# First layer of a fused two-block transformer: steps of the convolution and of the gate rows also advance behind the modulation units, and each chain has one step less

## Chip, cores, metric

The kernel runs on one core of one Trainium2 chip. The metric is the device time of one execution in microseconds (us). Before the change the median of three runs is 1377.7 us (1375.81 to 1378.25).

## What is computed

Two transformer blocks work on 256 tokens of width 1024, all in fp32. The first block has two mixers side by side (an attention of 8 heads and an mLSTM of 4 heads) and then a mixture of experts; the second is two layers of attention and a gated feed-forward. Both scale and shift their inputs by "modulation" vectors that come from a small matrix product of a condition `c`. What the change touches is the first block's mixer:

```python
mod = jax.nn.silu(c) @ w_ada[l] + b_ada[l]            # 12 units of 512 columns
sh1, sc1, g1, sh2, sc2, g2 = jnp.split(mod, 6, axis=-1)
h = modulate(x, norm1_g[l], sh1, sc1)
proj = h @ w_in[l]
q_a, k_a, v_a, qk_m, v_m, o_m, gates = jnp.split(proj, offs, axis=-1)
...
qk_m = jax.nn.silu(causal_conv(qk_m, conv_w[l], conv_b[l]))   # width 4
q_m, k_m = jnp.split(qk_m, 2, axis=-1)
gates = gates.astype(jnp.float32) + b_gate[l].astype(jnp.float32)
...
logf = jax.nn.log_sigmoid(f_pre); cum = jnp.cumsum(logf, axis=-1)   # running sums and maxima per head
...
hm = (hm * jax.nn.sigmoid(o_m.astype(jnp.float32))).astype(x.dtype)
```

## The kernel before

Five queues are written in program order: TensorE (PE), VectorE (DVE), ScalarE (ACT) and SyncE (SP, which issues the DMAs); GpSimd does nothing. Each engine runs its queue strictly in order, and waits on semaphores only where an operand or a buffer needs it. So the order in which the Python code emits instructions is the order on each engine.

All weights stream from HBM in units of 2 MB. A ring of four slots holds them; a slot is loaded again as soon as its unit has been consumed (`release`, or the last split of `stage`). The units of the first layer come in this order: modulation units `ada(0, n)` and projection units `U_IN + n` mixed.

A **projection unit** is multiplied with three fp32r products per tile (`mm3`). For that each of its eight slabs of 128 x 512 is split in two: ACT copies the high part (`ACTIVATE memr<-ring`), DVE subtracts for the low part (`TENSOR_TENSOR memr<-ring,memr`). `stage` does this up to four slabs ahead of the one in use (`NSP = 4`). PE then spends six matmuls of 512 columns (or twelve of 256) on the slab, and `slab_done` stages the next one.

A **modulation unit** (`ada_unit`) is 16 PE instructions `ps<-ring,csb`, one copy of the result to `rowb` by ACT, and later four transposes by PE (`ps<-cst,rowb`) and two small DVE instructions (`ada_close`). The transposes of the two open units are emitted behind the third slab of the next projection.

**Side work.** Other work that is not on the straight path is written as Python generators in the list `side`. `slab_done` advances each generator in it by one step, so one step's instructions stand on their queues behind each slab. In the first layer `side` holds `work()`, which goes through `jobs`: `conv(0)`, `conv(1)`, `gate_rows`, and later `mlstm`. `conv(u)` does four channel groups of 128 x 256 (one ACT instruction for the first tap, three on DVE, one SiLU per two). `gate_rows` is a chain of 14 small instructions on DVE and 5 on ACT over 4 x 256 or 4 x 128: biases, log-sigmoid (Exp, Ln), running sums and maxima, and at its end three `Exp` whose records are `gr_["e"]`. The first step of `mlstm` puts three PE transposes (`ps<-cst,mem`, 4 x 4) on PE's queue that wait for `gr_["e"]`. `drain()` emits at once whatever is left in `side`; it is called ahead of `mlstm`, behind the modulation units 7 and 8.

The order of the units around the change is: projection `U_IN + 3` (conv input 0), `U_IN + 4` (conv input 1), gates, modulation 4, `U_IN + 6` (output gate `omT`), modulation 5 and 6, `U_IN + 5` (`vm`), modulation 7 and 8, `drain()`, then `U_IN` (queries of the attention, called q slabs below) with the first steps of `mlstm` behind its slabs.

ACT holds one set of function tables at a time; `use_tables` loads the other set where a function needs it (`ACT_TABLE_LOAD`): SiLU and Tanh are in one, Exp and Ln in the other.

Of the kernel before, what the change touches and what calls it, by code (L numbers as in the profile page):

```python
# [165 lines left out]
def program(nc, t, dbg=None):  # L166
    vt, sc, te, sy, gp = nc.vector, nc.scalar, nc.tensor, nc.sync, nc.gpsimd
    ctx = ExitStack()
    with ctx:
# [154 lines left out]
        side = []  # L324
# [22 lines left out]
        def slab_done(z, rec):  # L347
            sp_free[z] = [rec]
            st["used"] += 1
            stage()  # L350
            for g in list(side):
                if next(g, StopIteration) is StopIteration:
                    side.remove(g)

        for slot in range(RING):
            load_unit(slot, [])
# [42 lines left out]
        def ada_mm(i, n):  # L399

            w, ld = unit("cols")
            src = csb[:, 0 if i == 0 else 1, :, :]
            b, ps, fr = PB.take()
            for k in range(8):
                j = k % 4
                r = mm(ps[32 * j:32 * j + 32, :], src[:, k, :], w[:, k, :], k < 4, k >= 4,
                       after=([ld, cs_r[0 if i == 0 else 1]] + fr) if k == 0 else ())
            release(r)
            ada_made.append((i, n, b, ps, r))
# [11 lines left out]
        def ada_unit(i, n):  # L421

            if len(ada_open) == 2:
                ada_close()
            ada_mm(i, n)
            ada_copy()
# [36 lines left out]
        def project(x2, x_r, evac, order=tuple(range(8))):  # L463

            bk = [PB.take(), PB.take()]
            for kk, k in enumerate(order):
                w, ld, z = slab()
                for tt in range(2):
                    s = slice(128 * tt, 128 * tt + 128)
                    r = mm3(bk[tt][1][:, :], (x2[0][:, k, s], x2[1][:, k, s]), w, kk == 0, kk == 7,  # L470
                            after=bk[tt][2] + [ld, x_r[k]])
                slab_done(z, r)
                if kk == 2:
                    ada_close(True)
            outs = []
            for tt in range(2):
                v = evac(tt, bk[tt][1], [r])
                PB.give(bk[tt][0], [v])
                outs.append(v)
            return outs, r  # L480
# [18 lines left out]
        def project_T(x2, x_r, c1, c2):  # L499
            out = []  # L500
            for _ in project_T_steps(x2, x_r, c1, c2, out):
                pass
            return out

        def silu(dst, src, after):
            use_tables(SILU)
            return A(sc.activation, dst, src, ACT.Silu, after=after)
# [272 lines left out]
        def conv(u, copies):  # L780
            prev, tap = None, {}

            def first(c):
                tap[c] = A(sc.activation, qmT[:, c, :], cT[:, c, 0:256], ACT.Identity, bias=cols[:, C_CB + c:C_CB + c + 1],
                           scale=cols[:, C_CW + 4 * c:C_CW + 4 * c + 1], after=[copies[c % 4 // 2], pad])

            first(4 * u)
            yield
            for c in range(4 * u, 4 * u + 4):
                r = tap[c]  # L790
                for j in (1, 2, 3):
                    r = V(vt.scalar_tensor_tensor, out=qmT[:, c, :], in0=cT[:, c, j:j + 256],
                          scalar=cols[:, C_CW + 4 * c + j:C_CW + 4 * c + j + 1], in1=qmT[:, c, :], op0=ALU.mult, op1=ALU.add,
                          after=[r])
                    if j == 1:
                        if c < 4 * u + 3:
                            first(c + 1)
                        yield
                yield
                if c % 2:  # L800
                    s = qmT[:, c - 1:c + 1, :]
                    conv_r[c] = conv_r[c - 1] = silu(s, s, [prev, r])
                prev = r
# [19 lines left out]
        def gates():  # L823
            b, ps, fr = PB.take()
            for k in range(8):
                r = mm3(ps[0:36, 0:256], (wg2[0][:, k, :], wg2[1][:, k, :]), (h2[0][:, k, :], h2[1][:, k, :]),
                        k == 0, k == 7, after=fr + wg_r + [h2_r[k]])
            return b, ps, r

        def gate_rows(b, ps, r):  # L830
            r1 = V(vt.tensor_scalar, rw[:, IG, :], ps[0:4, 0:256], bg[:, 0:1], None, ALU.add, after=[r, ld_rows])
            r2 = V(vt.tensor_copy, rw[:, FP, :], ps[32:36, 0:256])
            PB.give(b, [r1, r2])
            r2 = V(vt.tensor_scalar, rw[:, FP, :], rw[:, FP, :], bg[:, 1:2], None, ALU.add, after=[r2])
            r = V(vt.tensor_scalar, rw[:, T1, :], rw[:, FP, :], -1.0, None, ALU.mult, after=[r2])
            r = V(vt.tensor_tensor, rw[:, T1, :], rw[:, T1, :], rw[:, FP, :], ALU.max, after=[r])
            yield
            use_tables(LOG_EXP)
            r = A(sc.activation, rw[:, T1, :], rw[:, T1, :], ACT.Exp, scale=-1.0, after=[r])
            r = A(sc.activation, rw[:, T1, :], rw[:, T1, :], ACT.Ln, bias=1.0, scale=1.0, after=[r])  # L840
            yield
            r = V(vt.scalar_tensor_tensor, out=rw[:, T2, :], in0=rw[:, FP, :], scalar=0.0, in1=rw[:, T1, :],
                  op0=ALU.min, op1=ALU.subtract, after=[r])
            yield
            for c in range(2):
                s = slice(128 * c, 128 * c + 128)
                rc = V(vt.tensor_tensor_scan, rw[:, CU, s], cst[0:4, K_ONE:K_ONE + 128], rw[:, T2, s], 0.0, ALU.mult,
                       ALU.add, after=[r, ld_c1])
            yield
            ru = V(vt.tensor_tensor, rw[:, UU, :], rw[:, IG, :], rw[:, CU, :], ALU.subtract, after=[rc, r1])  # L850
            r = V(vt.tensor_tensor_scan, rw[:, MM, 0:128], rw[:, UU, 0:128], rw[:, UU, 0:128], 0.0, ALU.max, ALU.max,
                  after=[ru])
            yield
            r = V(vt.tensor_tensor, m1, rw[:, CU, 127:128], rw[:, MM, 127:128], ALU.add, after=[r])
            rn = V(vt.tensor_scalar, nml, rw[:, MM, 127:128], -1.0, None, ALU.mult)
            r = V(vt.tensor_tensor_scan, rw[:, MM, 128:256], rw[:, UU, 128:256], rw[:, UU, 128:256], m1, ALU.max,
                  ALU.max, after=[r])
            gr_["rM"] = r
            yield
            r = V(vt.tensor_tensor, rw[:, EM, :], rw[:, CU, :], rw[:, MM, :], ALU.add, after=[r])  # L860
            yield
            gr_["e"] = [A(sc.activation, rw[:, EM, :], rw[:, EM, :], ACT.Exp, scale=-1.0, after=[r]),
                        A(sc.activation, rw[:, WP, 0:128], rw[:, UU, 0:128], ACT.Exp, bias=nml, scale=1.0, after=[rn]),
                        A(sc.activation, rw[:, WI, 128:256], rw[:, MM, 128:256], ACT.Exp, bias=m1, scale=-1.0), ru]
            yield
# [202 lines left out]
        copies = conv_copy(0, *conv_out)  # L1068
        jobs = []

        def work():
            while jobs:
                g, n = jobs[0]
                for _ in range(n):
                    if next(g, StopIteration) is StopIteration:
                        jobs.pop(0)
                        break
                yield

        gate_weights()  # L1080
        jobs += [(conv(0, copies), 1)]
        side.append(work())
        bk, r = project_T(h2, h2_r, 256, 128)
        copies = conv_copy(1, bk, r)
        jobs += [(conv(1, copies), 1), (gate_rows(*gates()), 1)]
        if not side:
            side.append(work())
        ada_unit(0, 4)
        bk, r = project_T(h2, h2_r, 256, 128)
        for j in range(2):  # L1090
            o = omT[:, 2 * j:2 * j + 2, :]
# [2 lines left out]
            PB.give(bk[j][0], [ra])  # L1094
            om_r.append(V(vt.tensor_scalar, o, o, 0.5, 0.5, ALU.mult, ALU.add, after=[ra]))
        ada_unit(0, 5)
        ada_unit(0, 6)
        vm_r += project(h2, h2_r, lambda tt, ps, dep: A(sc.activation, vm[:, tt, :], ps[:, :], ACT.Copy, after=dep))[0]
        ada_unit(0, 7)
        ada_unit(0, 8)  # L1100
        drain()
        use_tables(LOG_EXP)
        jobs.append((mlstm(), 1))
        if not side:
            side.append(work())

# [36 lines left out]
        wo1, _ = fold_out(c2_, c_r, (4, 5, 6, 7), 0, 0, x_r)  # L1143
# [452 lines left out]
        for i in (1, 2):  # L1596
# [181 lines left out]
            else:  # L1778
# [64 lines left out]
                _, h2_last = project(h2, h2_r, q_ev(1))  # L1843
# [17 lines left out]
            wo1, _ = fold_out(c2_, c_r, (0, 1, 2, 3), i, 0, x_r)  # L1861
# [16 lines left out]
            for n in range(11):  # L1878
                bk, ff_last = project_T(h2, h2_r, 128, 256)
                for m in range(2):  # L1880
                    f = 2 * n + m
                    z = f % 4
                    b, ps, _ = bk[m]
# [25 lines left out]
            x_r, _ = fold_out(act2, f_r, tuple(range(22)), i, 1, x_r, nm)  # L1909
# [124 lines left out]
```

How the kernel before makes its waits and increments, by code:

```python
def emit(q, ops, seen):  # L133
    for o in ops:
        if o[0] == "wait":
            r = o[1]
            if seen.get(r.sem.name, 0) < r.value:
                q.eng.wait_ge(r.sem, r.value)
                seen[r.sem.name] = r.value
        elif o[0] == "op":
            ins = o[1](*o[2], **o[3])
            if o[4].marked:
                ins.then_inc(o[4].sem, o[4].step)
        elif o[0] == "load":
            q.eng.reg_load(o[1], o[2])
        else:
            with q.eng.If_cmp(o[1], o[2], "IS_GT"):
                emit(q, o[3], dict(seen))
```

## Time and profile before

| quantity | value |
|---|---|
| median of three runs | 1377.7 us (1375.81 to 1378.25) |
| profiled execution: its time | 1377.22 us |
| its span in the trace | 1375.4 us |
| PE busy | 1153.6 us (84%) |
| DVE busy | 611.5 us (44%) |
| ACT busy | 540.8 us (39%) |
| read from HBM | 394.97 MB, 288 GB/s over the span |
| mean granted TensorE clock | 0.944 of full speed |

The span begins with the first instruction and ends with the last; about 1.8 us of the profiled execution's time lie outside it. The mean share says little by itself: the program has stages with different limits, and the stage of the change ends some 100 us after the start.

### The profile page before, as it was taken

How to read it: one execution, taken by the hardware profiler on the slowest of the kernel's cores; microseconds unless marked ns; L12 is line 12 of the kernel's file. 1: busy time of each engine (PE TensorE's matmuls, PEld its weight loads, DVE VectorE, ACT ScalarE, POOL GpSimd, SP SyncE). 2: the span in 40 equal slices, each digit the busy share in tenths (PEclk: the TensorE clock that was granted, in tenths of full speed). 3: DMA queues.
4: the chain of work that ended last, by engine and by line, in shares of the span. 5: the costliest groups of instructions: out<-in, count | busy, mean ns of one | idle time of the engine just before them, and what ended most of it. 6: DMA issues, size and time to landing. Idle time of an engine off the chain costs nothing.

```text
span 1375.4 us, 22370 instructions
## 1 busy us (share of the span) xinstructions
PE 1153.6 (84%) x9627; PEld 917.0 (67%) x9627; DVE 611.5 (44%) x1363; ACT 540.8 (39%) x1203; POOL 0.2 (0%) x4
## 2 busy tenths in 40 slices
PE   6989998857475666657589989999999989999997
PEld 4867678534243443424257757999998758899997
DVE  4564664201110110101165765665555855655554
ACT  4554553211101111101155665555554654655553
POOL 0000000000000000000000000000000000000000
PEclk9999998989788889978899999999999999999999
DMA  9895847899999999999978655555546655655520
GB/s 390 345 356 223 355 186 294 341 427 427 428 426 426 424 427 427 426 426 428 426 299 307 235 194 198 231 184 184 185 153 230 228 215 184 245 184 184 184 93 31
DMA packets 29569, 397.53 MB, mean 289 GB/s; under 512 B 3480, under 2 KB 4888, under 8 KB 5400
## 3 DMA queue, kind: packets, MB, share of 16 engines
q1 hardware_dynamic: 29032, 395.72, 72.1%
q8 instruction: 78, 1.28, 0.4%
q10 hardware_dynamic: 432, 0.30, 0.1%
q14 instruction: 27, 0.22, 0.0%
HBM read 394.97 MB, written 1.05 MB: 288 GB/s over the span
## 4 chain that ended last, share of the span: by engine, by line
PE 61%; DMA 20%; DVE 10%; ACT 7%; issue 2%; SPq 0%; ACTq 0%; DVEq 0%
PE ps L141 61%; DMA mem<-in_w 13%; DMA ring<-in_w 5%; DVE mem L141 5%; DVE memr L141 3%; ACT mem L141 3%; ACT memr L141 3%; DMA ring<-in_wpk 1%; DVE small L141 1%; DMA posi<-in_pos 1%; ACT L141 0%; ACT rowb L141 0%; DVE x L141 0%; SPq L141 0%; DVE mcol L141 0%
## 5 line engine op out<-in xcount | busy, mean ns | idle before, releaser
L141 PE MATMUL ps<-memr 128*128 128x256 f32 (+1 forms) x4680 | 670.6, 303 | 17.9 <-DVE memr L141 17.9
L141 PEld LDWEIGHTS ps<-memr 128*128 128x128 f32 x4680 | 612.4, 193 | 62.5 <-DVE memr L141 27.8
L141 DVE TENSOR_TENSOR memr<-ring,memr 128x512 fp32r<-128x512 f32 x440 | 297.7, 690 | 247.0 <-ACT memr L141 243.6
L141 PE MATMUL ps<-mem 128*32 128x256 f32 (+5 forms) x2360 | 299.1, 421 | 86.8 <-DMA ring<-in_w 34.9
L141 ACT ACTIVATE memr<-ring 128x512 fp32r<-128x512 f32 x440 | 268.2, 627 | 221.6 <-PE ps L141 214.6
L141 PEld LDWEIGHTS ps<-mem 128*32 128x32 f32 (+3 forms) x2360 | 185.9, 150 | 158.6 <-issue 106.7
L141 ACT ACTIVATE mem<-ps 128x256 f32<-128x256 f32 (+5 forms) x307 | 121.3, 407 | 417.4 <-PE ps L141 415.4
L141 PE MATMUL ps<-ring,mem 128*32 128x256 f32 x1408 | 150.4, 428 | 40.5 <-DMA mem<-in_w 35.7
L141 DVE TENSOR_TENSOR mem<-mem,ps 128x256 f32<-128x256 f32 (+1 forms) x76 | 31.7, 418 | 270.3 <-ACT mem L141 270.3
L141 PEld LDWEIGHTS ps<-ring,mem 128*32 128x32 f32 x1408 | 72.8, 122 | 78.9 <-issue 53.3
L141 DVE COPY mem<-ps 32x256 f32<-32x256 f32 (+2 forms) x81 | 38.2, 471 | 118.7 <-PE ps L141 117.7
L141 PE MATMUL ps<-cst,mem 128*128 128x128 f32 (+2 forms) x267 | 47.7, 283 | 47.8 <-DVE mem L141 43.5
L141 PEld LDWEIGHTS ps<-cst,mem 128*128 128x128 f32 (+2 forms) x267 | 31.5, 148 | 77.3 <-DVE mem L141 62.5
L141 PE MATMUL ps<-ring,csb 128*32 128x512 f32 x560 | 66.7, 603 | 1.8 <-DMA ring<-in_wpk 1.8
L141 PE MATMUL ps<-mem,cst 128*128 128x256 f32 (+3 forms) x158 | 45.5, 399 | 14.0 <-ACT mem L141 10.6
L141 DVE SCALAR_TENSOR_TENSOR x<-ps,mcol,x 128x256 f32<-128x256 f32 x72 | 34.0, 480 | 28.9 <-PE ps L141 28.5
L141 ACT ACTIVATE mem<-x 128x256 f32<-128x256 f32 (+1 forms) x52 | 22.2, 433 | 60.0 <-DVE x L141 57.2
L141 ACT ACTIVATE memr<-mem 128x256 fp32r<-128x256 f32 (+1 forms) x58 | 24.6, 425 | 45.7 <-DVE mem L141 45.7
L141 PEld LDWEIGHTS ps<-mem,cst 128*128 128x128 f32 (+1 forms) x158 | 24.9, 200 | 26.1 <-ACT mem L141 15.7
L141 PEld LDWEIGHTS ps<-ring,csb 128*32 128x32 f32 x560 | 15.4, 110 | 36.0 <-issue 32.2
L141 DVE TENSOR_TENSOR memr<-mem,memr 128x256 fp32r<-128x256 f32 (+1 forms) x58 | 25.2, 434 | 28.6 <-ACT memr L141 28.6
L141 DVE TENSOR_TENSOR mem<-mem 128x256 f32<-128x256 f32 (+3 forms) x76 | 30.4, 415 | 2.3 <-ACT mem L141 0.6
(91 smaller groups left out, 379.7 us busy)
## 6 DMA issues: line engine op xcount, KB each, us to landing
ring<-in_wpk SPq DMA_DIRECT2D x89, 2048.0 KB, 8.1
mem<-in_w SPq DMA_DIRECT2D x52, 2048.0 KB, 34.4
ring<-in_w SPq DMA_DIRECT2D x44, 2048.0 KB, 36.5
mem<-in_wpk SPq DMA_DIRECT2D x1, 2048.0 KB, 10.4
ring<-in_wpk SPq DMA_DIRECT2D x2, 1024.0 KB, 5.3
x<-in_x SPq DMA_DIRECT2D x2, 512.0 KB, 5.7
out_dram<-mem SPq DMA_DIRECT2D x4, 256.0 KB, 2.2
cst<-in_cst SPq DMA_DIRECT2D x1, 944.0 KB
```

Source lines behind the costliest of these rows:

```text
L141: ins = o[1](*o[2], **o[3])
```

## The change

`slab_done` called the generators of `side` itself; this is now a function `step_side`. It is also called once behind each of the modulation units 4, 5, 6 and 7 of the first layer. `conv` loses its first `yield`, so that the first tap and the first DVE instruction of a chain come in one step. `work` goes on to the next job in the same step when a job has ended, where it used to give the step up. No arithmetic is added or removed.

```diff
@@ slab_done
             stage()
-            for g in list(side):
-                if next(g, StopIteration) is StopIteration:
-                    side.remove(g)
+            step_side()
+
+        def step_side(n=1):
+
+            for _ in range(n):
+                for g in list(side):
+                    if next(g, StopIteration) is StopIteration:
+                        side.remove(g)
@@ conv
             first(4 * u)
-            yield
             for c in range(4 * u, 4 * u + 4):
@@ work and its callers
         def work():
             while jobs:
-                g, n = jobs[0]
-                for _ in range(n):
-                    if next(g, StopIteration) is StopIteration:
-                        jobs.pop(0)
-                        break
-                yield
+                if next(jobs[0], StopIteration) is StopIteration:
+                    jobs.pop(0)
+                else:
+                    yield
...
         ada_unit(0, 4)
+        step_side()
         bk, r = project_T(h2, h2_r, 256, 128)
...
         ada_unit(0, 5)
+        step_side()
         ada_unit(0, 6)
+        step_side()
         vm_r += project(h2, h2_r, lambda tt, ps, dep: A(sc.activation, vm[:, tt, :], ps[:, :], ACT.Copy, after=dep))[0]
         ada_unit(0, 7)
+        step_side()
         ada_unit(0, 8)
         drain()
```

What this does to the queues. **PE's queue** is the same before and after, instruction for instruction. These are its rows from the modulation units 5 and 6 to the second q slab; `ps<-cst,mem 128x4` are the first transposes of `mlstm`:

```order
L141 MATMUL ps<-ring,csb 32x512 x16
L141 MATMUL ps<-memr 128x512 x18
L141 MATMUL ps<-cst,rowb 128x128 x8
L141 MATMUL ps<-memr 128x512 x30
L141 MATMUL ps<-ring,csb 32x512 x16
L141 MATMUL ps<-memr 128x512 x6
L141 MATMUL ps<-cst,mem 128x4 x3
L141 MATMUL ps<-memr 128x512 x6
```

**ACT's queue before**, from the `vm` slabs 5 to 8 to the q slabs 5 to 8; `mem<-mem 4x256` and `mem<-mem,small 4x128` are the functions of `gate_rows`, the single `mem<-mem 128x512` is the last SiLU of the convolution, `mem<-ps 128x512 x2` are the copies of `vm`:

```order
L141 ACTIVATE memr<-ring 128x512 x4
L141 ACTIVATE mem<-mem 128x512
L141 ACTIVATE memr<-ring 128x512 x2
L141 ACT_TABLE_LOAD
L141 ACTIVATE mem<-mem 4x256 x2
L141 ACTIVATE memr<-ring 128x512 x2
L141 ACTIVATE mem<-ps 128x512 x2
L141 ACTIVATE rowb<-ps 128x512 x2
L141 ACTIVATE mem<-mem 4x256
L141 ACTIVATE mem<-mem,small 4x128 x2
L141 ACTIVATE memr<-ring 128x512 x4
```

ACT's queue now, from the `vm` slabs 1 to 4; here the first `mem<-ps 128x512 x2` are the two Tanh of `omT`, the second the copies of `vm`:

```order
L141 ACTIVATE memr<-ring 128x512 x4
L141 ACTIVATE mem<-mem 128x512
L141 ACTIVATE mem<-ps 128x512 x2
L141 ACTIVATE rowb<-ps 128x512
L141 ACT_TABLE_LOAD
L141 ACTIVATE mem<-mem 4x256 x2
L141 ACTIVATE rowb<-ps 128x512
L141 ACTIVATE memr<-ring 128x512 x5
L141 ACTIVATE mem<-mem 4x256
L141 ACTIVATE mem<-mem,small 4x128 x2
L141 ACTIVATE memr<-ring 128x512 x3
L141 ACTIVATE mem<-ps 128x512 x2
```

The table load with the first Exp and Ln moved from behind the second q slab to between the copies of the modulation units 5 and 6, ahead of the `vm` slabs 5 to 8. The last three Exp moved from behind the copies of `vm` and of the modulation units 7 and 8 to behind the first q slab (the fifth of the `x5`).

**DVE's queue before**, from the first two q slabs on; all rows of 4 partitions belong to `gate_rows`:

```order
L141 TENSOR_TENSOR memr<-ring,memr 128x512 x2
L141 TENSOR_SCALAR mem<-ps,bg 4x256
L141 COPY mem<-ps 4x256
L141 TENSOR_SCALAR mem<-mem,bg 4x256
L141 TENSOR_SCALAR mem<-mem 4x256
L141 TENSOR_TENSOR mem<-mem 4x256
L141 TENSOR_TENSOR memr<-ring,memr 128x512 x2
L141 SCALAR_TENSOR_TENSOR mem<-mem 4x256
L141 TENSOR_TENSOR memr<-ring,memr 128x512
```

DVE's queue now, from the fourth `vm` slab on; `mem<-mem 128x512 x2` scales `omT`:

```order
L141 TENSOR_TENSOR memr<-ring,memr 128x512
L141 TENSOR_SCALAR mem<-ps,bg 4x256
L141 COPY mem<-ps 4x256
L141 TENSOR_SCALAR mem<-mem,bg 4x256
L141 TENSOR_SCALAR mem<-mem 4x256
L141 TENSOR_TENSOR mem<-mem 4x256
L141 TENSOR_SCALAR mem<-mem 128x512 x2
L141 SCALAR_TENSOR_TENSOR mem<-mem 4x256
L141 TENSOR_TENSOR memr<-ring,memr 128x512
L141 SCALAR_TENSOR_TENSOR mem<-cst,mem 4x128 x2
L141 TENSOR_TENSOR memr<-ring,memr 128x512
L141 TENSOR_TENSOR mem<-mem 4x256
```

`gate_rows` now begins before the first `vm` slab is used, and its DVE instructions are spread over the `vm` slabs; the last of them stands ahead of the first q slab. SP's queue has the same DMAs in the same order.

## Rows read from the trace of the kernel before

**Rows 1.** The page: the span, and the chain that ended last, by engine.

```profile
span 1375.4 us, 22370 instructions
...
PE 61%; DMA 20%; DVE 10%; ACT 7%; issue 2%; SPq 0%; ACTq 0%; DVEq 0%
```

**Rows 2.** Timeline of PE: start us, duration us, instructions; in brackets idle time before, releaser.

```profile
79.33 4.42 PE L141 MATMUL ps<-memr 128*128 128x512 f32 x18
83.58 1.03 PE L141 MATMUL ps<-cst,rowb 128*128 128x128 f32 x8
84.37 7.09 PE L141 MATMUL ps<-memr 128*128 128x512 f32 x30
91.39 3.64 PE L141 MATMUL ps<-ring,csb 128*32 128x512 f32 x32
94.96 1.65 PE L141 MATMUL ps<-memr 128*128 128x512 f32 x6
100.82 0.32 PE L141 MATMUL ps<-cst,mem 4*128 4x4 f32 x3 [4.20 <-ACT mem L141]
101.06 2.49 PE L141 MATMUL ps<-memr 128*128 128x512 f32 x6
103.35 1.06 PE L141 MATMUL ps<-cst,mem 128*128 128x128 f32 x4
104.06 2.09 PE L141 MATMUL ps<-memr 128*128 128x512 f32 x6
106.07 1.15 PE L141 MATMUL ps<-mem,cst 4*128 4x128 f32 x8
```

**Rows 3.** Timeline of ACT, the same columns.

```profile
77.82 1.06 ACT L141 ACTIVATE mem<-ps 128x512 f32<-128x512 f32 x2
78.78 1.28 ACT L141 ACTIVATE rowb<-ps 128x512 f32<-128x512 f32 x2
...
90.46 1.15 ACT L141 ACTIVATE memr<-ring 128x512 fp32r<-128x512 f32 x2 [3.25 <-DMA ring<-in_wpk]
91.63 1.28 ACT L141 ACT_TABLE_LOAD   x1
93.82 0.86 ACT L141 ACTIVATE mem<-mem 4x256 f32<-4x256 f32 x2 [0.91 <-DVE mem L141]
...
99.56 0.41 ACT L141 ACTIVATE mem<-mem 4x256 f32<-4x256 f32 x1 [1.93 <-DVE mem L141]
99.89 0.68 ACT L141 ACTIVATE mem<-mem,small 4x128 f32<-4x128 f32 x2
```

**Rows 4.** Timeline of DVE, the same columns.

```profile
78.43 0.91 DVE L141 TENSOR_SCALAR mem<-mem 128x512 f32<-128x512 f32 x2 [0.73 <-ACT mem L141]
...
91.12 0.69 DVE L141 TENSOR_TENSOR memr<-ring,memr 128x512 fp32r<-128x512 f32 x1 [3.72 <-ACT memr L141]
91.73 0.47 DVE L141 TENSOR_SCALAR mem<-ps,bg 4x256 f32<-4x256 f32 x1
...
99.12 0.41 DVE L141 TENSOR_TENSOR mem<-mem 4x256 f32<-4x256 f32 x1
```

**Rows 5.** Stretches: start:end, length, busy us per engine, granted clock, DMA share, GB/s.

```profile
43.00:96.50 53.50, 53.50 (x398) 43.54 (x396) 32.94 (x70) 32.23 (x57) 0.00 (x0) 0.99 0.86 332
101.70:105.00 3.30, 3.30 (x11) 2.69 (x10) 1.02 (x4) 0.63 (x1) 0.00 (x0) 0.50 1.01 432
242.00:247.00 5.00, 4.81 (x75) 3.01 (x74) 2.75 (x19) 2.19 (x5) 0.00 (x0) 1.00 0.04 16
250.00:690.00 440.00, 283.94 (x3419) 172.40 (x3408) 52.59 (x141) 53.12 (x143) 0.00 (x0) 0.86 1.01 427
```

**Rows 6.** Waits of SP's queue from 0 to 260 us: total, times, longest.

```profile
SPq L141 <- PE ps L141: 131.3, 23, 17.5
```

**Rows 7.** The DMA issued at 95.1 us (unit `U_IN + 1`): issue, and time to landing.

```profile
L141 SPq DMA_DIRECT2D ring<-in_wpk x1: 328/328/328, 95.1 to 95.1; - x1
...
DMA to landing us min/median/max: 12.9/12.9/12.9
```

More of the change, by code:

```diff
@@ L1072, in work @@
             while jobs:
-                g, n = jobs[0]
-                for _ in range(n):
-                    if next(g, StopIteration) is StopIteration:
-                        jobs.pop(0)
-                        break
-                yield
+                if next(jobs[0], StopIteration) is StopIteration:
+                    jobs.pop(0)
+                else:
+                    yield
         gate_weights()
-        jobs += [(conv(0, copies), 1)]
+        jobs.append(conv(0, copies))
         side.append(work())
@@ L1084, in program @@
         copies = conv_copy(1, bk, r)
-        jobs += [(conv(1, copies), 1), (gate_rows(*gates()), 1)]
+        jobs += [conv(1, copies), gate_rows(*gates())]
         if not side:
@@ L1102, in program @@
         use_tables(LOG_EXP)
-        jobs.append((mlstm(), 1))
+        jobs.append(mlstm())
         if not side:
```

## The prediction

> **What bounds the kernel now.** I first read the page's chain of work that ended last: PE carries 61% of the span, DMA 20%, DVE 10%, ACT 7% [rows 1]. So there is no single bound, and the stage of the change has to be read by itself. The busy time by stretches shows two regimes. Up to about 247 us the first layer's mixer runs, with PE busy nearly all the time. Then the experts' weights stream: from 250 to 690 us the DMA engines are busy all the time at 427 GB/s while PE is busy 284 of 440 us [rows 5]. After that PE leads again.
>
> The change touches 60 to 100 us. PE's timeline there is closed but for one hole: the first q slab starts at 94.96 and takes 1.65 us, and then PE stands for 4.20 us, until 100.82, when the three small transposes of `mlstm` run [rows 2]. Those wait for ACT, namely for the last Exp of `gate_rows`.
>
> Why is that Exp late? Follow it back through the timelines of ACT and DVE. ACT stands 3.25 us until 90.46, for the DMA of the q unit [rows 3]; DVE stands 3.72 us until 91.12 behind it, for the same slab [rows 4]. Only behind that slab's split, at 91.73, does the first instruction of `gate_rows` run, although the gates' products have been in PSUM since the matmuls ahead of modulation unit 4. From there the chain goes 91.73 (DVE), 93.82 (Exp, Ln, behind a table load at 91.63), DVE again until 99.12 + 0.41 = 99.53, and three Exp from 99.56 to 99.89 + 0.68 = 100.57 [rows 3, 4]. 0.25 us later PE goes on. So the hole is the chain of `gate_rows`, 8.8 us long, started only 3.2 us before PE has finished the modulation units 7 and 8 at 94.96.
>
> The hole has a second price. The granted clock is 0.50 from 101.7 to 105 us [rows 5], the 1.2 GHz level, right behind the pause. The two q slabs there advance PE by 103.35 - 101.06 = 2.29 and 106.07 - 104.06 = 2.01 us, and four transposes by 104.06 - 103.35 = 0.71 [rows 2]. At full clock six such matmuls advance it by (91.39 - 84.37) / 5 = 1.40, and eight transposes by 84.37 - 83.58 = 0.79, so four by 0.40 [rows 2].
>
> **The change, part by part.**
>
> PE's own instructions and their order are unchanged: 0 us. All that can move PE is when it waits.
>
> *The hole.* `gate_rows` now starts on DVE behind the split of the fourth `vm` slab. Before, DVE was free there from 78.43 - 0.73 = 77.70 [rows 4]. Its first five instructions took 93.82 - 91.73 = 2.1 us, so they end near 79.8. On ACT I take the Tanh where it was, 77.82, the copy of modulation unit 5 from 78.78 to 79.42 (half of 1.28), then 1.28 for the table load, 0.86 for Exp and Ln: 81.6 [rows 3]. The DVE steps that follow are 0.4 us pieces between the splits of the `vm` slabs 5 to 8 and end near 88. The last three Exp stand on ACT behind the split of the first q slab, which waits for the DMA until 90.46. They run from 91.1 to 91.1 + 1.1 = 92.2. PE needs them at 94.96 + 1.65 = 96.6. The margin is 4.4 us, so the pause of 4.20 us goes completely.
>
> *The clock.* What did PE before the clock fell? It paused. From 43 to 96.5 us it is busy without a wait and the granted clock is 0.99 [rows 5]; without the pause that goes on, so I expect 1.00 here. Gain: (2.29 - 1.40) + (2.01 - 1.40) + (0.71 - 0.40) = 1.8 us.
>
> Bounds for the second term: 0 if the low stretch only falls on other matmuls, 1.8 if it goes.
>
> *What the moved instructions push back.* Here the cover must be named. Between the copies of the modulation units 5 and 6 ACT now has the table load, Exp and Ln. The copy of unit 6 therefore ends at 81.6 + 0.64 = 82.2. Behind it stand the ACT splits of `vm` slabs 5 to 8, and PE's eight transposes wait for it; they run at 83.58 [rows 2], a margin of 1.4 us. The high part of `vm` slab 5 is then ready at 82.2 + 0.6 = 82.8 (half of the row at 90.46) and DVE's part 0.7 later, 83.5 [rows 3, 4]. PE comes to it at 84.37 + 1.40 = 85.8 [rows 2], a margin of 2.3 us. Slabs 6 to 8 wait for PE to free a buffer, as before. So this costs 0 as long as ACT is less than 1.4 us later than worked out. With that cover gone every further us is a us of PE.
>
> The Trainium skill, "ScalarE: Activation LUTs", section "What ACT_TABLE_LOAD costs", speaks against the new place: a switch of table set costs about 2.66 us, of which the load is 1.28 and the rest a drain. By that rule, an estimate, the copy of unit 6 would end near 83.6, just where the transposes need it, and the change would still gain nearly the same. This trace shows the load with 1.28 us [rows 3], and the wait behind it there is for DVE.
>
> *Behind the hole.* PE now comes to everything after 106.07 some 6 us earlier. The q slabs 2 to 4 are split at once behind the three Exp and the `vm` copies, so they are ready by 95. DVE's copy that `mlstm`'s second step needs now stands behind the split of the fifth q slab, which PE frees at 96.6: it runs at about 98, and PE needs the product that follows it after about 103. The next unit, `U_IN + 1`, was issued at 95.1, a time that PE sets ahead of the hole, and lands at 108.0 [rows 7]. Its first slab was split at 112 us and would be at 106: ACT will stand up to 2 us there. The four slabs split ahead are more than 10 us of PE work, so PE feels nothing: 0 us, at most 2.
>
> *The conv chains.* The step that `conv` loses and the steps behind modulation units 4 and 5 only move ACT and DVE pieces of 0.4 to 0.6 us by one slab, while PE has no pause between 43 and 96.5 us [rows 5]: 0.
>
> *Does the gain reach the end?* The experts' stream is bound by DMA, so a gain ahead of it counts only if the stream starts earlier. SP waits 131.3 us for PE up to 260 us [rows 6], and from 242 to 247 us the DMA engines are at a share of 0.04 [rows 5]: the loads wait for PE to free slots, not the other way round. So the whole stream shifts with PE, and behind 690 us PE leads again.
>
> **Sum.** 4.20 + 1.8 = 6.0 us. The profiled execution took 1377.2, 0.5 less than the median shown. From 1377.7 that gives **1371.7 us**, or -0.44%. A change of 0.2% (2.8 us) is about what a measurement of this kernel can tell from no change.
>
> **Rivals.**
>
> *The pause goes, but not the low clock, or a low stretch lands elsewhere* (chance 0.15). The clock is also low in stretches of the experts' part (0.86 on average from 250 to 690 us) [rows 5], and everything shifts against them. Time: 1377.7 - 4.2 = 1373.5. With one more low stretch, about 2 us, 1375.5. The Trainium skill, "TensorE: Matmul & The Clock Gate", section "What's actually happening", calls where a slow start falls run-variable; the mechanism is the same as this rival's. The same could give 2 us more: 1369.7 (0.07).
>
> *The gain is hidden in the DMA-bound stream* (0.11). For it speaks the share of 1.01 over 440 us [rows 5]; against it the idle DMA just ahead. It would give 1377.7.
>
> *A new wait on ACT ahead of PE's transposes at 83.58 takes the hole's place* (0.05), the one that ends on the other side. If the table load, Exp and Ln, or the DVE steps that they wait for, hold the copy of unit 6 beyond 83.58, PE pauses there, and a low clock follows, another 1.8 us. The change is even when the copy ends near 83.58 + 6.0 - 1.8 = 87.8, and slower by 0.2% from 90.6 on; that is 8.4 us later than I work out. A lesser form, 3 us late, gives 1376.5. The slow form gives 1380.5 or more.
>
> *The gate chain is still late*, since the last Exp still stand behind the DMA that lands at 90.46: it would take a landing more than 4.4 us later. I put this under the hidden gain, with the same time.
>
> **From cases to numbers.** The forecast has 0.62. Forecast and both clock rivals hold 0.84; the clock rival with an extra low stretch is the one part of them above 1374.9, about 0.03, and goes to no change. Faster 0.82, same 0.14, slower 0.04. The range reaches from the extra low stretch saved (1369.7, rounded down to 1369.0 for the spread of the runs) to one more of them (1375.5), and leaves out about 0.18.
>
> **What the changed profile would show.** Right: no wait of PE at the small transposes near 96.6 us; granted clock 1.0 from there on; the Exp of 4 x 256 near 91; the same SP idle pattern and the 427 GB/s stretch some 6 us earlier; a wait of ACT of up to 2 us near 106 for the DMA of `U_IN + 1`. Wrong: PE idle ahead of `ps<-cst,rowb` near 83.6 or ahead of `vm` slab 5 near 85.8; the stream starting no earlier; or new stretches of clock 0.5 between 106 and 250 us.

## The result, and the profile after

The changed kernel is faster: the ratio of its time to that of the kernel before is 0.9959 (95% interval 0.9948 to 0.9971), -5.6 us on the 1377.7 us that the prediction started from; 6.0 us were forecast. In 12 runs each the medians are 1374.64 us (1370.2 to 1376.4) and, for the kernel before, 1379.79 us (1375.81 to 1383.2). The two medians lie 5.15 us apart; where the text speaks of a gain it goes by the ratio. The median of the kernel before is now 2.1 us above the 1377.7 of its first three runs (the nine later ones have 1381.5), and that is most of why the absolute forecast of 1371.7 is low by 3 us while the difference fits. The profiled execution of the changed kernel took 1370.2 us, span 1368.3.

PE's timeline of the changed kernel around the old hole (start us, duration, instructions; a bracket would give idle time before and its releaser) answers to [rows 2]:

```profile
84.24 1.03 PE L141 MATMUL ps<-cst,rowb 128*128 128x128 f32 x8
85.03 7.09 PE L141 MATMUL ps<-memr 128*128 128x512 f32 x30
92.05 3.64 PE L141 MATMUL ps<-ring,csb 128*32 128x512 f32 x32
95.62 1.65 PE L141 MATMUL ps<-memr 128*128 128x512 f32 x6
97.20 0.34 PE L141 MATMUL ps<-cst,mem 4*128 4x4 f32 x3
97.48 1.68 PE L141 MATMUL ps<-memr 128*128 128x512 f32 x6
98.99 0.60 PE L141 MATMUL ps<-cst,mem 128*128 128x128 f32 x4
99.35 1.64 PE L141 MATMUL ps<-memr 128*128 128x512 f32 x6
100.91 1.15 PE L141 MATMUL ps<-mem,cst 4*128 4x128 f32 x8
```

No bracket stands behind the three small transposes: PE does not wait. This execution is 0.66 us late at the start of the stage (84.24 against 83.58), so compare distances: from the first q slab to the eight matmuls of `mlstm` it was 106.07 - 94.96 = 11.11 us and is 100.91 - 95.62 = 5.29. That is 5.82 us less. The stretches of the changed kernel (start:end, length, busy us per engine, granted clock, DMA share, GB/s) show the clock behind the place, and the experts' stream:

```profile
97.20:101.00 3.80, 3.80 (x21) 2.91 (x20) 1.92 (x4) 1.26 (x2) 0.00 (x0) 1.00 1.01 414
...
250.00:690.00 440.00, 285.49 (x3361) 174.18 (x3361) 54.58 (x146) 54.93 (x148) 0.00 (x0) 0.86 1.01 426
```

The clock is 1.00 where it was 0.50 [rows 5]. ACT's timeline of the changed kernel answers to [rows 3]:

```profile
78.99 0.60 ACT L141 ACTIVATE rowb<-ps 128x512 f32<-128x512 f32 x1
79.61 1.28 ACT L141 ACT_TABLE_LOAD   x1
80.90 0.87 ACT L141 ACTIVATE mem<-mem 4x256 f32<-4x256 f32 x2
81.67 0.57 ACT L141 ACTIVATE rowb<-ps 128x512 f32<-128x512 f32 x1
...
92.20 0.63 ACT L141 ACTIVATE memr<-ring 128x512 fp32r<-128x512 f32 x1 [4.86 <-DMA ring<-in_wpk]
92.73 0.40 ACT L141 ACTIVATE mem<-mem 4x256 f32<-4x256 f32 x1
93.04 0.68 ACT L141 ACTIVATE mem<-mem,small 4x128 f32<-4x128 f32 x2
...
108.34 0.63 ACT L141 ACTIVATE memr<-ring 128x512 fp32r<-128x512 f32 x1 [2.34 <-DMA ring<-in_wpk]
```

Three things are to be seen. The table load, Exp and Ln now stand ahead of the copy of modulation unit 6, which ends at 81.67 + 0.57 = 82.24, 2.0 us before the first of PE's eight transposes at 84.24. The wait for the q unit's DMA is still there (4.86 us), but only one slab and the last three Exp are behind it; they end at 93.72, and PE comes at 97.20. And ACT waits 2.34 us, until 108.34, for the next unit's DMA, without a wait of PE behind it.

Where does the gain go? PE's and SP's timelines of the two executions give the position of fixed points in the program. In this ordinary table the last column is after minus before:

| point | before | after | difference |
|---|---|---|---|
| first q slab starts | 94.96 | 95.62 | +0.66 |
| eight matmuls of `mlstm` | 106.07 | 100.91 | -5.16 |
| router's matmuls | 226.07 | 220.94 | -5.13 |
| SP's issue that begins the first 35 us DMA on the chain | 284.01 | 278.44 | -5.57 |
| first modulation unit behind the experts | 695.96 | 689.98 | -5.98 |
| end | 1375.4 | 1368.3 | -7.1 |

Nearly all of the shift is made in one place, and it is carried through the 440 us in which DMA sets the pace. Of what comes on top, 0.4 us lie between the router's matmuls and the experts' first ones (16.66 us in place of 17.09), where another part of the work meets a low clock; the 1.1 us behind 690 us I have not traced. Such pieces differ from one execution to the next, and only the ratio over many runs counts.

### The profile page after: what moved, and what is told of

Same layout as the page of the kernel before. It is cut to its first block, busy times and chain, and to the rows that moved or that the text cites. A ratio compares the mean times of both kernels' runs of the same rounds, so it can differ in the third digit from the quotient of the medians.

```text
span 1368.3 us, 22371 instructions
## 1 busy us (share of the span) xinstructions
PE 1151.4 (84%) x9627; PEld 913.0 (67%) x9627; DVE 610.5 (45%) x1363; ACT 540.0 (39%) x1203; POOL 0.2 (0%) x4
## 4 chain that ended last, share of the span: by engine, by line
PE 62%; DMA 20%; DVE 9%; ACT 6%; issue 2%; SPq 0%; DVEq 0%; ACTq 0%
PE ps L141 62%; DMA mem<-in_w 13%; DMA ring<-in_w 5%; DVE mem L141 4%; DVE memr L141 3%; ACT mem L141 3%; ACT memr L141 3%; DMA ring<-in_wpk 2%; DVE small L141 1%; ACT rowb L141 0%; ACT L141 0%; DVE x L141 0%; SPq L141 0%; DVE mcol L141 0%; ACT small L141 0%
## 5 line engine op out<-in xcount | busy, mean ns | idle before, releaser
L141 PE MATMUL ps<-ring,mem 128*32 128x256 f32 x1408 | 153.5, 434 | 39.6 <-DMA mem<-in_w 34.8
```

The lines of the kernel that those rows point to most:

```text
L141: ins = o[1](*o[2], **o[3])
```

## The experiments

Each kernel is compared with the kernel before on the same chip; the rows come from several chips, so two of them are compared by their ratios. A summary first: D is the distance from the first q slab's start to the eight matmuls of `mlstm` on PE, as above; the forecast ratio is 1 - (11.11 - D) / 1377.7.

| kernel | pause of PE | D | ratio from D | ratio measured (95%) |
|---|---|---|---|---|
| before | 4.20 | 11.11 | | 1 |
| one_step | 3.28 | 10.18 | 0.9993 | 0.9992 (0.9982 to 1.0002) |
| before_filled | 1.22 | 9.95 | 0.9992 | 0.9983 (0.9971 to 0.9994) |
| two_steps | 1.35 | 6.68 | 0.9968 | 0.9967 (0.9956 to 0.9978) |
| steps_only | 0.74 | 6.07 | 0.9963 | 0.9965 (0.9953 to 0.9976) |
| chains_only | 0 | 5.29 | 0.9958 | 0.9956 (0.9940 to 0.9971) |
| after | 0 | 5.29 | 0.9958 | 0.9959 (0.9948 to 0.9971) |
| after_pe_work | 0 | 11.19 | 1.0001 | 0.9994 (0.9982 to 1.0005) |

D is read from one execution of each kernel, the ratio comes from many. Every measured interval, about 1.5 us to either side, holds the ratio that this one distance gives, so a stretch of 11 us accounts for the change of 1375 as closely as these runs can tell. `after_loads4`, whose pause lies ahead of the q slabs (its D is 5.29), is not in the table.

### The low clock priced by itself: before_filled

```diff
 def mlstm():
     b, ps, fr = PB.take()
+    for q in range(15):
+        r = mm(ps[:, :], h2[0][:, q % 8, 0:128], h2[0][:, 0:2, :].rearrange("p a b -> p (a b)"), True, True,
+               after=fr if q == 0 else ())
```

> The kernel before with 15 matmuls of 128x512 whose product nobody reads, on PE's queue ahead of the three small transposes, in the hole (15 x 0.233 = 3.5 us of the 4.20 us pause). The gate chain stays late. My theory (the pause is 4.2 us, and the low clock behind it costs a separate 1.8 us because PE paused): the transposes still run at about 100.8 us, but the granted clock stays at 1.00 behind them, and the two q slabs advance PE by about 1.4 to 1.5 us each in place of 2.29 and 2.01; time 1.8 us below the kernel before, ratio 0.9987. Rival (the low clock belongs to that place in time and not to the pause): clock 0.5 near 102 to 105 us again, ratio 1.000.

PE's timeline of this kernel:

```profile
101.17 0.32 PE L141 MATMUL ps<-cst,mem 4*128 4x4 f32 x3 [1.22 <-ACT mem L141]
101.42 1.68 PE L141 MATMUL ps<-memr 128*128 128x512 f32 x6
102.93 0.60 PE L141 MATMUL ps<-cst,mem 128*128 128x128 f32 x4
103.28 1.64 PE L141 MATMUL ps<-memr 128*128 128x512 f32 x6
104.85 1.15 PE L141 MATMUL ps<-mem,cst 4*128 4x128 f32 x8
```

The chain of `gate_rows` is untouched, and the transposes run as late as before, by 0.4 us even later (101.17 - 94.90 = 6.27 us behind the first q slab, against 100.82 - 94.96 = 5.86, for the q unit's DMA landed later). But the same groups behind them now take 104.85 - 101.42 = 3.43 us, where [rows 2] has 106.07 - 101.06 = 5.01: 1.6 us, at a granted clock of 1.00 from 101.4 to 105 us. The 1.8 of the sum measured 1.6; with the later transposes D shrinks by 1.16 us in this execution. Ratio 0.9983, the forecast 0.9987 within its interval, and the rival's 1.000 outside it. So the low clock is a price of the pause and not of the place, and here useless matmuls saved it.

### Does a us of PE here reach the end? after_pe_work

```diff
 def mlstm():   # in the changed kernel
     b, ps, fr = PB.take()
+    for q in range(26):
+        r = mm(...)    # the same matmuls
```

> The changed kernel with 26 more matmuls of 128x512 whose product nobody reads, ahead of the three small transposes: 26 x 0.233 = 6.1 us of PE work at full clock, where the hole was. My theory (time of PE ahead of the experts' stream reaches the end one to one): 6.1 us above the changed kernel, so ratio to the kernel before 0.9959 + 0.0044 = 1.0003. Rival (the DMA-bound stream hides what happens ahead of it): no change, ratio 0.996.

Measured 0.9994, that is 0.0035 or 4.8 us above the changed kernel's 0.9959; its PE distance is 11.19, 5.9 us longer. The point value is a little low, but 1.0003 lies in the interval (0.9982 to 1.0005) and 0.996 does not. The stream of the experts does not hide the time ahead of it: the rival by which the gain would be lost is out. That every single us comes through is more than the interval, 1.6 us to either side, can show.

### The cover on ACT used up: after_loads4

```diff
         ada_unit(0, 5)
         step_side()
+        for _ in range(2):
+            A(sc.preload_act_table_set, SILU)
+            A(sc.preload_act_table_set, LOG_EXP)
         ada_unit(0, 6)
```

> The changed kernel with four more function table loads on ACT ahead of modulation unit 6, to use up the cover that the moved Exp and Ln left. By the trace's 1.28 us each they hold ACT 5.1 us: the copy of unit 6 ends at 82.2 + 5.1 = 87.4 in place of 82.2, PE's eight transposes wait about 3.1 us from 84.3, and the low clock behind that pause costs up to 1.8 us: 4.9 us above the changed kernel, ratio to the kernel before 0.9994. Rival (ACT has much more cover there, so it costs nothing): ratio 0.996. Second rival (each load with a drain of its own, 2.66 us): a pause of 8.6 us, ratio above 1.003.

Timelines of this kernel, ACT first and then PE:

```profile
78.72 0.87 ACT L141 ACTIVATE mem<-mem 4x256 f32<-4x256 f32 x2
79.61 5.15 ACT L141 ACT_TABLE_LOAD   x4
84.77 0.60 ACT L141 ACTIVATE rowb<-ps 128x512 f32<-128x512 f32 x1
```

```profile
82.11 0.60 PE L141 MATMUL ps<-cst,rowb 128*128 128x128 f32 x4
85.42 0.66 PE L141 MATMUL ps<-cst,rowb 128*128 128x128 f32 x4 [2.71 <-ACT rowb L141]
85.83 8.68 PE L141 MATMUL ps<-memr 128*128 128x512 f32 x30
94.44 3.64 PE L141 MATMUL ps<-ring,csb 128*32 128x512 f32 x32
```

The pause appears at the transposes, as in the prediction's slower rival, but only ahead of the second four: 2.71 us (forecast 3.1). The first four, of modulation unit 5, run at 82.11 without a wait. The prediction let all eight wait for the copy of unit 6; only four do, so the cover was 0.4 us larger than it said, and that is the 0.4 us that this pause is shorter. Behind it the clock is low again, 0.57 from 86 to 90 us, and the 30 matmuls of the `vm` slabs advance PE by 94.44 - 85.83 = 8.61 us in place of 92.05 - 85.03 = 7.02. Together 4.3 us, and the ratio is 0.9989, 4.1 us above the changed kernel (forecast 4.9; the interval 0.9976 to 1.0001 leaves out 0.996). The prediction put the even point at a copy that ends near 87.8; here it ends at 84.77 + 0.60 = 85.37, which is 86.8 on the timeline of the kernel before (whose transposes run 1.47 us later), 1.0 us short of that; the measured ratio leaves 1.5 us of gain, and an even time is just inside the interval. So the cover on ACT was real and small, and the moved table load sat inside it. The four loads take 5.15 us, 1.29 each, and the next instruction starts 0.01 us later: the drain that the Trainium skill names with each switch ("ScalarE: Activation LUTs", "What ACT_TABLE_LOAD costs", 2.66 us in all) does not show in this trace, neither ahead of the four loads (0.02 us) nor behind them.

### Which half of the change does it? chains_only and steps_only

chains_only has the edits of `conv` and `work` and none of the `step_side()` calls:

```diff
         ada_unit(0, 4)
-        step_side()
...
         ada_unit(0, 5)
-        step_side()
         ada_unit(0, 6)
-        step_side()
...
         ada_unit(0, 7)
-        step_side()
```

> Only the edits of conv and of work: one step less per chain, the next job begins in the step in which the last ended; no steps behind modulation units. The last three Exp stand behind the split of the second or third q slab and ahead of the copies of vm, near 93 to 94 us, before PE needs them at 96.6. My theory (what counts is only whether the Exp are done by 96.6): the whole gain, ratio 0.996, no wait at the small transposes. Rival (the steps behind the modulation units are what closes the hole): ratio 0.999 to 1.000, part of the pause remains.

The ratio is as forecast, 0.9956, with no wait at the transposes. The Exp are later than I wrote, though:

```profile
91.37 2.19 ACT L141 ACTIVATE memr<-ring 128x512 fp32r<-128x512 f32 x4 [3.88 <-DMA ring<-in_wpk]
95.61 0.41 ACT L141 ACTIVATE mem<-mem 4x256 f32<-4x256 f32 x1 [2.05 <-DVE mem L141]
95.93 0.68 ACT L141 ACTIVATE mem<-mem,small 4x128 f32<-4x128 f32 x2
```

ACT waits 2.05 us for the DVE part of the chain, which still has to run between the splits of the q slabs. They end at 96.61, and PE comes at 97.35: 0.7 us of margin, where the full change has 97.20 - 93.72 = 3.5.

steps_only has the calls, and undoes the other half:

```diff
             first(4 * u)
+            yield
...
                 if next(jobs[0], StopIteration) is StopIteration:
                     jobs.pop(0)
-                else:
-                    yield
+                yield
```

> Only the calls behind the modulation units 4 to 7; conv keeps its first yield and work gives a step up between jobs. The last three Exp stand between the copies of modulation units 7 and 8, near 95.4 us. My theory: no pause or one under 0.5 us, granted clock 1.00, ratio 0.996, the same as with the other half of the change alone (0.9956) and as with both. Rival (the halves add up, each bringing a part): ratio near 0.998.

A pause of 0.74 us is left, the clock stays at 1.00 behind it, and the ratio is 0.9965. The pause is above the 0.5 us that I allowed: ACT waits 1.82 us for DVE, as in chains_only, and the last Exp end at 96.72, not near 95.4. By their point values the halves bring 4.8 and 6.1 us, and together 5.6: they do not add up, and the rival's 0.998 lies outside the interval. Once the Exp are in time, more earliness buys nothing but margin.

### How the pause depends on the lateness: one_step and two_steps

The kernel before with one call, or two, of `step_side()` behind modulation unit 6 and nothing else:

```diff
         ada_unit(0, 6)
+        step_side()
```

> The kernel before with a single extra step of the side work, behind modulation unit 6. gate_rows starts one slab earlier on DVE, but its Exp and Ln still stand behind the DMA of the q unit, and its last three Exp behind the copy of modulation unit 8. My theory (the pause is the lateness of that chain, so it shrinks by what one step brings): the last Exp near 98.3 us, a pause of about 1.7 us in place of 4.2, and a low clock only if so short a pause brings one (the 1.08 us pause near 171 us in the kernel before brings none). Gain 2.5 us without a low clock of 0.7 with it kept, up to 4.3 if it goes too: ratio 0.997 to 0.9995. Rival (the hole closes at the first step): ratio 0.996.

> The same with two steps behind modulation unit 6. Now the table load, Exp and Ln stand ahead of the split of the first q slab, that is ahead of the wait for its DMA. My theory: the last Exp at about 96.7 us, a pause under 0.5 us, granted clock 1.00: nearly the whole gain, ratio 0.9960 to 0.9965. Rival (each step moved earlier counts alike, so two steps of the six or so bring a third): ratio 0.9985.

PE's timeline of one_step, then of two_steps:

```profile
98.62 0.31 PE L141 MATMUL ps<-cst,mem 4*128 4x4 f32 x3 [3.28 <-ACT mem L141]
98.87 1.70 PE L141 MATMUL ps<-memr 128*128 128x512 f32 x6
100.37 1.05 PE L141 MATMUL ps<-cst,mem 128*128 128x128 f32 x4
101.08 2.87 PE L141 MATMUL ps<-memr 128*128 128x512 f32 x6
103.88 1.15 PE L141 MATMUL ps<-mem,cst 4*128 4x128 f32 x8
```

```profile
96.49 0.32 PE L141 MATMUL ps<-cst,mem 4*128 4x4 f32 x3 [1.35 <-ACT mem L141]
96.74 1.67 PE L141 MATMUL ps<-memr 128*128 128x512 f32 x6
...
100.17 1.15 PE L141 MATMUL ps<-mem,cst 4*128 4x128 f32 x8
```

One step shortens the pause by 0.9 us only, not by the 2.5 that I had worked out, and the low clock stays (0.54 from 101 to 104 us): ratio 0.9992. Five of the chain's 14 DVE instructions (from 86.05 us) now ran ahead of the q unit's DMA, but the table load (89.86), the first Exp and all that follows them were still behind it. Two steps put them ahead of that wait: the pause falls to 1.35 us (forecast under 0.5), the clock stays at 1.00, and 4.5 us of the 5.6 are there. In the ratio one_step came out inside the range that I gave, two_steps (0.9967) at its edge, the range (0.9960 to 0.9965) being inside its interval; in the pause both expectations were too short. By D the second step brings 3.5 us and the first 0.9: what counts is which side of the DMA wait the chain's instructions stand on, and whether the pause brings a low clock.

### A version that beats both: after_again, after_fill_router, after_fill_all

before_filled suggests filling pauses whose cause can't be removed. `filler(n)` is n fp32 matmuls whose product nobody reads, two records each in the trace (the comments in this cut are mine, not the kernel's):

```diff
+        def filler(n):
+            b, ps, fr = PB.take()
+            for q in range(n):
+                r = mm(ps[:, 0:256], ident, cst[:, 0:256], True, True, after=fr + [ld_c1] if q == 0 else ())
+            PB.give(b, [r])
...
         rB_r = nm.close()                 # ahead of the router, in both
+        filler(4)
...
         conv_step = project_T_steps(...)  # near 22 us, in after_fill_all alone
+        filler(6)
...
             ada_close(True)               # end of first_half, near 38 us, in after_fill_all alone
+            filler(4)
```

> The changed kernel once more, beside the two kernels with filled pauses, as their measure. Ratio to the kernel before 0.996 again, no wait at the small transposes, granted clock 1.00 behind them.

> The changed kernel with four fp32 matmuls of 128x256, whose product nobody reads, in the 1.98 us pause of PE ahead of the router's matmuls (about 4 x 0.45 = 1.8 us). Theory (a pause of PE costs its length and then a low clock; filling it saves the second part): the router's 32 matmul records take under 5 us in place of 6.58, and the granted clock from 222 to 228 us is 1.00 in place of 0.50; 1.5 to 3 us less than the changed kernel, ratio to the kernel before 0.994 to 0.995. Rival (the four matmuls are longer than the pause, or other pauses near there bring the low clock anyway): ratio 0.996 or above.

> The same with the pauses of 3.44 us at 22 us (six matmuls) and of 2.33 us at 38 us (four) filled too. Theory: the granted clock stays at 1.00 from 24 to 30 and from 41 to 45 us, 2 us less from each if PE is the limit there: ratio to the kernel before 0.991 to 0.993. Rival (DVE and ACT, which make these stages' operands, are the limit from 24 to 45 us, so a faster PE only waits): the ratio of the kernel with the router's pause filled alone.

The changed kernel beside them: 0.9955 (0.9942 to 0.9969). With the router's pause filled: 0.9950 (0.9937 to 0.9964), which by time can't be told from it. With all three: 0.9930 (0.9917 to 0.9944), median 1371.90 us against 1375.34 and 1382.08; all five of its runs (1369.17 to 1373.15) are below all five of the changed kernel (1374.45 to 1376.26), and its mean granted clock is 0.946 to 0.951 in them where the changed kernel has 0.940 to 0.944. So filling all three pays 3.4 us, at the upper end of the ratio that I expected. PE's timeline at the start of the program and at the router, of after_again and then of after_fill_all; then two rows of after_fill_router at the router, and one of two_steps, which has no filler, at the start:

```profile
25.32 8.47 PE L141 MATMUL ps<-memr 128*128 128x256 f32 x48 [3.44 <-DVE memr L141]
...
41.07 21.80 PE L141 MATMUL ps<-memr 128*128 128x256 f32 x168 [2.33 <-DVE memr L141]
...
221.34 6.41 PE L141 MATMUL ps<-w,mem 128*128 128x40 f32 x32 [1.99 <-ACT mem L141]
227.55 3.65 PE L141 MATMUL ps<-cst,mem 128*128 128x128 f32 x16
231.90 2.31 PE L141 MATMUL ps<-mem,cst 128*128 128x32 f32 x10 [0.69 <-DVE small L141]
```

```profile
25.52 1.69 PE L141 MATMUL ps<-memr 128*128 128x256 f32 x12 [0.85 <-DVE memr L141]
27.71 1.69 PE L141 MATMUL ps<-memr 128*128 128x256 f32 x12 [0.50 <-DVE memr L141]
29.90 3.13 PE L141 MATMUL ps<-memr 128*128 128x256 f32 x24 [0.50 <-DVE memr L141]
...
40.31 20.30 PE L141 MATMUL ps<-memr 128*128 128x256 f32 x168 [0.61 <-DVE memr L141]
...
216.94 1.89 PE L141 MATMUL ps<-cst 128*128 128x256 f32 x8
219.09 3.76 PE L141 MATMUL ps<-w,mem 128*128 128x40 f32 x32 [0.26 <-ACT mem L141]
222.68 1.94 PE L141 MATMUL ps<-cst,mem 128*128 128x128 f32 x16
227.00 1.27 PE L141 MATMUL ps<-mem,cst 128*128 128x32 f32 x10 [2.37 <-DVE small L141]
```

```profile
219.88 3.77 PE L141 MATMUL ps<-w,mem 128*128 128x40 f32 x32 [0.26 <-ACT mem L141]
223.47 3.54 PE L141 MATMUL ps<-cst,mem 128*128 128x128 f32 x16
```

```profile
40.07 20.30 PE L141 MATMUL ps<-memr 128*128 128x256 f32 x168 [2.33 <-DVE memr L141]
```

At the router of after_fill_all the filler runs 1.89 us inside the pause, the router's records take 3.76 in place of 6.41 us and the transposes 1.94 in place of 3.65. Of these 4.4 us, 1.7 go into a longer wait for DVE (2.37 against 0.69): DVE's routing chain is the next bound there. But the filler did not hold the clock in after_fill_router: there the records take 3.77 us, and then the clock falls all the same, to 0.52 from 223.5 to 227 us (0.72 from 222 to 228, where I had expected 1.00), and the transposes take 3.54 us. In the changed kernel and in after_again the clock is 0.50 and 0.51 from 222 to 228.

At the start of the program the faster PE waits for DVE 0.50 us each near 27 and 29 us, so the rival had a part. The 168 matmuls from 40 us on take 1.5 us less than in after_again. That is no proof for the filler ahead of them: in four of the eleven traces without it (one_step, two_steps, after_pe_work, after_loads4) they take 20.29 or 20.30 us too, at a granted clock of 1.00 from 41 to 45 us, behind the same pause of 2.33 us. From 24 to 30 us no trace without filler has more than 0.72, and after_fill_all has 1.00. That filling all three pauses pays is thus shown by the runs; how much each filler brings is not.

## Why the prediction was right, point by point

- **The hole.** The forecast was 4.20 us, because the last Exp would be done 4.4 us before PE needs them. They were done 3.5 us before; the q unit's DMA landed later in that execution (ACT went on at 92.20 - 0.66 = 91.5, where the old timeline has 90.46). The pause is gone, for the reason given.
- **The clock.** The forecast was 1.8 us; before_filled measured 1.6 by itself. The term is 0.2 us too large because the sum took 1.40 us for six matmuls at full clock, from a closed run of 30; beside the transposes they advance PE by 98.99 - 97.48 = 1.51 and 100.91 - 99.35 = 1.56. The sum of both terms measured 5.82 on PE's timeline, and 5.6 in time, against 6.0.
- **What the moved instructions push back.** The forecast was 0, with the copy of unit 6 ending at 82.2, 1.4 us ahead of the transposes. It ended 2.0 us ahead of them (82.24, which is 81.6 on the old timeline). after_loads4 showed that this wait is the one that opens next, and that only four of the eight transposes stand behind it: the prediction's reading was too strict there.
- **Behind the hole.** The forecast of a wait of ACT of up to 2 us near 106 came as 2.34 us from 106.0 to 108.34, and cost PE nothing.
- **The conv chains.** Forecast 0. PE is busy without a wait from 43 to 97.1 us in the changed kernel (54.10 of 54.10 us).
- **The gain reaches the end.** The table of fixed points shows -5.16, -5.57 and -5.98, and the DMA's idle stretch ahead of the experts' stream comes earlier too (no bytes from 239 to 242 us, where the kernel before has its lull from 242 to 247 us); after_pe_work shows it in the other direction.
- **Which rivals fell.** The hidden gain, by after_pe_work. The new wait on ACT, by the changed kernel's own timeline. That a low stretch lands elsewhere did happen in part, and the prediction had named it as a sign of being wrong: the router's 32 records took 5.41 us before, 6.58 and 6.41 in the two traces of the changed kernel, because the low stretch behind the router's pause begins within 1 us of the first record in the changed kernel (0.74 from 221 to 222 us, 0.50 after) and 2 us behind it in the kernel before (0.95 from 227 to 228, then 0.50). It is the old low stretch on other matmuls, not a new one (the granted clock from 106 to 250 us is 0.96 in the kernel before and in the changed one), and over the runs it left no more than the interval. Where a low stretch falls is luck in a single execution; that the ratio came out this near to the forecast, 5.6 against 6.0, is closer than the interval of 1.6 us can promise.

## What to carry to other kernels

When an engine stands behind a short chain, look for what stands ahead of the chain in its own queues: here 14 small DVE instructions, handed out one step per slab, came up just behind a weight load that they did not need. Moving side work pays little as long as most of the chain stays behind such a wait (0.9 us for the first step), and much once it crosses it (3.5 us for the second); once the chain is done before its consumer comes, more earliness buys margin only. Price a PE pause as its length plus a low clock that may follow it, and where the cause can't be moved, try a few useless matmuls, short enough to end inside the pause, and judge them by the times of several runs, since a single trace can show a full clock there without them.

## What the runs showed of the hardware

At the small transposes and at those of modulation unit 6, pauses of PE of 0.74, 1.22 and 1.35 us left the granted clock at 1.00 in these traces; those of 2.71, 3.28 and 4.20 us were followed by 0.50 to 0.57, the lower of the two levels for all or most of the stretch, and 1.6 us were lost each time (5.01 us for the groups behind the pause in place of 3.43 in the kernel before and in one_step, 8.61 in place of 7.02 in after_loads4). But it is not the length alone. The pause of 1.98 or 1.99 us ahead of the router was followed by a low stretch in all the traces without filler there; it begins at the earliest just ahead of the router's first record (steps_only, from 220 to 221 us at 0.63) and at the latest some 2.5 us behind it (two_steps, from 222 to 223 us at 0.85). The pause of 2.33 us near 38 us was followed by 1.00 from 41 to 45 us in four traces and by 0.57 to 0.79 in seven. With all three pauses filled the clock is 1.00 from 22 to 45 and from 218 to 228 us in the one trace that there is, and the kernel is 0.25% faster over five runs; with the router's alone filled it was 1.00 through the router's records and low behind them.
